# Twenty-eight copies of old value rows move from the prompt attention to the routing's queries, and from GpSimd to ScalarE

## The reference

```
p = modulate(rmsnorm(x)) @ w_in                 # q, k, v of two attention groups
oa = differential attention (softmax pair)      # prompt: causal; samples: paged past
ob = dilated window attention, three windows    # prompt; samples: past of 2048 rows
x += gate * ([norm(oa), ob] @ w_o)
q = modulate(rmsnorm(x)) @ peer_wq              # PEER: 8 heads, two halves of 128
s = q . keys; top 16 of each half, top 16 of the sums   # the routing
x += gate * sum over chosen experts of softmax * gelu(x . u[e]) * v[e]
y = rmsnorm(x)
k_win_sample = concat(state_k_win, kb)[:, 4:]   # the window state, moved by 4 rows
v_win_sample = concat(state_v_win, vb)[:, 4:]
```

## Time and profile before

| | |
|---|---|
| median of 3 runs | 4041.88 us (4033.55 to 4056.06) |
| the profiled execution | 4036.62 us |
| its span in the trace | 4034.8 us |
| busy: TensorE, weight load, VectorE, ScalarE, GpSimd | 82%, 72%, 69%, 34%, 42% |
| `prompt_attn`, 399.49 to 719.24 us | TensorE busy 240.7, VectorE 207.4, ScalarE 182.2 of 319.8 us; DMA 0.53 |
| queries, sparse turns, 1251.5 to 1387.4 us | TensorE busy 107.0 of 135.9 us; VectorE 0; DMA 0.34 |
| queries, dense turns, 1387.4 to 1537.5 us | TensorE busy 133.0, VectorE 133.7 of 150.1 us; DMA 0.34 |

### The profile page before, as it was taken

How to read it: one execution, slowest core, us unless ns; L and a number is a source line. 1 busy time by engine, 2 the same in 40 slices (tenths; PEclk the granted TensorE clock), 3 DMA queues, 4 the chain that set the end, 5 groups by cost and what they waited for, 6 DMA issues and landing times. The chain is left out here.

```text
span 4034.8 us, 59078 instructions
## 1 busy us (share of the span) xinstructions
PE 3311.0 (82%) x20585; PEld 2890.3 (72%) x20585; DVE 2778.2 (69%) x5881; ACT 1357.6 (34%) x3190; POOL 1709.0 (42%) x1341
## 2 busy tenths in 40 slices
PE   6999688566686892666589999999999999999994
PEld 3677455211376792555489999999999999999993
DVE  3223676100231199999779998999999889999885
ACT  3010466000221111887633333333333333333331
POOL 1010000000212441888765665665565565565560
PEclk7999799777788996776699999999999999999997
DMA  6632546999422331787598998998988988898983
GB/s 232 221 124 74 172 148 212 357 412 406 161 72 77 99 115 42 200 240 205 141 329 318 330 325 303 326 331 311 326 319 314 334 316 314 320 322 307 328 300 148
DMA packets 389552, 1001.89 MB, mean 248 GB/s; under 512 B 187044, under 2 KB 232975, under 8 KB 325688
## 3 DMA queue, kind: packets, MB, share of 16 engines
q1 hardware_dynamic: 323768, 491.18, 35.9%
q0 software_dynamic: 62656, 469.86, 32.2%
q10 hardware_dynamic: 2944, 38.77, 2.6%
HBM read 914.75 MB, written 152.04 MB: 264 GB/s over the span
## 5 line engine op out<-in xcount | busy, mean ns | idle before, releaser
L2174 DVE CUSTOM_DVE_ANT_0 e_uv<-e_uv,e_h 128x1024 f32<-128x1024 f32 x416 | 721.7, 1735 | 73.8 <-DMA e_uv<-peer_uv,k_g_idx 73.1
L2243 POOL DMA_INDIRECT e_uv<-peer_uv,k_g_idx x416 | 521.1, 1253 | 540.4 <-DVE e_pY L2186 496.8
L1475 PE MATMUL e_po<-e_ph,e_vh 128*128 128x320 f32 x2048 | 646.3, 316 | 59.2 <-DVE k_OT L2218 55.1
L1475 PE MATMUL e_pa<-k_hi_d,e_uh 128*128 128x320 f32 x2048 | 638.4, 312 | 50.7 <-POOL e_ul L2234 37.5
L1476 PE MATMUL e_po<-e_pl,e_vh 128*128 128x320 f32 x2048 | 633.3, 309 | 0.0
L1477 PE MATMUL e_po<-e_ph,e_vl 128*128 128x320 f32 x2048 | 633.3, 309 | 0.0
L1477 PE MATMUL e_pa<-k_hi_d,e_ul 128*128 128x320 f32 x2048 | 633.2, 309 | 0.0
L1476 PE MATMUL e_pa<-k_lo_d,e_uh 128*128 128x320 f32 x2048 | 633.1, 309 | 0.0
L2186 DVE SCALAR_TENSOR_TENSOR e_pY<-e_uv,e_wts,e_pY 128x1024 f32<-128x1024 f32 x412 | 526.0, 1277 | 0.0
L1475 PEld LDWEIGHTS e_po<-e_ph,e_vh 128*128 128x128 f32 x2048 | 384.8, 188 | 83.7 <-DVE k_OT L2218 71.3
L1475 PEld LDWEIGHTS e_pa<-k_hi_d,e_uh 128*128 128x128 f32 x2048 | 384.8, 188 | 62.0 <-issue 46.0
(11 more groups left out here) (305 smaller groups left out, 5889.7 us busy)
## 6 DMA issues: line engine op xcount, KB each, us to landing
k_kv<-kv_pages SPq DMA_DIRECT2D x128, 512.0 KB, 7.0
s_kv<-kv_state SPq DMA_DIRECT2D x32, 2048.0 KB
e_v<-peer_uv SPq DMA_DIRECT2D x128, 512.0 KB
e_u<-peer_ut SPq DMA_DIRECT2D x126, 512.0 KB, 6.1
s_g<-r_G SPq DMA_DIRECT2D x10, 4096.0 KB
k_OT<-s_g SPq DMA_DIRECT2D x128, 320.0 KB
v_win_sample<-state_v_win POOLq DMA_DIRECT2D x28, 1168.0 KB, 10.0
k_win_sample<-state_k_win ACTq DMA_DIRECT2D x28, 1168.0 KB
```

Source lines behind the costliest of these rows:

```text
L1475: nc.tensor.matmul(out, lhs_hi, rhs_hi, start=start, stop=False)
L2174: nc.vector.tensor_tensor_reduce(uv[:, r, 0:D], uv[:, r, 0:D], h[:], 1.0, 0.0, ALU.mult, ALU.add, dots[:, r:r + 1]).then_inc(row_dotted, 1)
L2243: nc.gpsimd.indirect_dma_start(uv[:, s % RING], None, io["peer_uv"], bass.IndirectOffsetOnAxis(ap=keep.g_idx[:, s:s + 1], axis=0),).then_i ...
```

## The change

GpSimd's program in `prompt_attn` falls away with its two semaphores. In the queries of `peer_route`, ScalarE issues share x of the values at the end of turn x, behind `scores_away(x - 1)`, for x from 0 to 27. Nobody waits for these until the end of `finish`, where SyncE already waited for the 28 of the keys and now waits for 56.

```diff
@@ prompt_attn
-        win_out = [nc.alloc_semaphore(f"a_win_out{u}") for u in range(2)]
...
-            @block.gpsimd
-            def _(pool):
-                with pool.Fori(0, WIN_SHARES // 2) as i:
-                    for u in range(2):
-                        copy_window(pool, io, "v", 2 * i + u).then_inc(win_out[u], 16)
-                        pool.wait_ge(win_out[u], 16 * i + 16)
@@ peer_route, ScalarE
                     queries_away(x)
                     if x:
                         scores_away(x - 1)
+                    if x < WIN_SHARES:
+                        copy_window(act, io, "v", x).then_inc(keep.win_out, 16)
                     if x in (NHC + 6, NHC + 11):
                         exps(ND if x == NHC + 6 else ND + 1)
@@ finish, SyncE
-                sp.wait_ge(keep.win_out, 16 * WIN_SHARES)
+                sp.wait_ge(keep.win_out, 2 * 16 * WIN_SHARES)
```

## The result

| | before | after |
|---|---|---|
| median | 4045.75 us (4 runs, 4033.55 to 4056.06) | 4181.97 us (4 runs, 4163.93 to 4200.73) |
| ratio | | 1.0338 (1.0271 to 1.0406) |
| profiled span | 4034.8 us | 4195.9 us |

The prediction was 4082 us, in a range of 4044 to 4122. The way was right, but the time lies outside the range: the loss is three to four times the one forecast. The profiled execution of after lies in the upper part of its runs, so its parts sum to 161 us, not to 136.

The account below looks back on a forecast made before the run. The queries were held bound by a ring of TensorE, GpSimd and the weights load. VectorE 53 us late less 10 gained gave +43 on 4036.62, 4079.6; plus 2, 4082 us, own range 4060 to 4105, with neighbours 4044 to 4122.

Parts of the forecast that it names:

- The gain: Prompt attention without its 28 copies: 6.4 us saved at the stage's end, 3.5 at its start, together 10 (6 to 13).
- The ring: Queries: TensorE waits for GpSimd, GpSimd for weights; 16.4 us per two sparse turns; a later load delays both equally.
- Eight engines for 6.7 us a share: Queries: each value share holds about 8 of 16 engines for 6.7 us and leaves the others free.
- h = 4 us: Queries: lateness of each weights load that waits for the rest of a share; 4 us, with 0 and 7.8 as ends.
- The meeting at 568 us: Prompt attention: an `a_qk` load meeting a copy landed after 14.7 us, its twin after 6.7 to 7.1; worst lateness 7.8.
- Turns 1 to 15: Sparse turns of the queries: 7 rounds, each 4.6 us longer including slower clock, 32 us in all.
- Turns 16 to 22: Queries: 3 rounds, each 5.0 us longer, 15 us; ScalarE's exponential of turn 22 and VectorE late by 47.
- Turns 22 to 27: Queries: 2.5 rounds, 12.5 us; exponential of turn 27 late by 59.5, VectorE by 53 after 6.4 of play.
- Turns 27 to 31: End of the queries: no share in turns 28 to 31, nothing added; first dense tile's load stays hidden.
- The load passes between the packets: Rival, queries: engines alternate, so the load loses one packet, 1.3 us; +5 in all, 4042 us; chance 0.16.
- The eight engines fill up: Rival, queries: 18.7 us of engine work against rounds of 16.4 to 17.4, queue runs behind; +91, 4128 us; chance 0.14.
- The share fills engines that are idle: Rival, queries: DMA at 0.34 leaves room, loads hardly late, not slower; 4027 to 4031 us without lateness; chance 0.08.

Follow-up runs that it names:

- e3: Kernel after with the same bytes in 32 shares of 511 rows of one sequence, each on sixteen engines; 4091.53 us, 1.0127 of before.
- e2: Kernel after with every second value share left out, 14 shares remaining; 4119.35 us, 1.0195 of before.
- e9: Kernel after with the shares issued by SyncE directly ahead of each turn's weights, instead of by ScalarE; 4127.23 us, 1.0226 of before.
- e4: Kernel after with 32 shares on sixteen engines, issued by SyncE directly behind each turn's weights; 4032.29 us, 0.9988 of before.
- e6: Kernel after with each share in 256 pieces of 4.7 KB instead of 40 of 30 KB, same eight engines; 4123.18 us, 1.0207 of before.

## Why the prediction was wrong

- **The gain.** 6.4 at the end and 3.5 at the start were forecast, 6.6 and 6.2 measured, and 3.8 more between, where nothing was forecast. At the start of the queries 11.7 us were left of the stage's 16.6, counted from the start of the prompt attention, where 10 was forecast. The two ends were rightly seen; that the sum came so near is partly luck, since 3.8 us unforeseen came in and 4.9 went again.
- **The ring.** That GpSimd waits for the weights and TensorE for GpSimd, and that a late load makes a round later by as much, is what the trace shows: the rounds took 15.6 us on average before and 30.3 after (turn 1 to turn 15), 14.7 more, and the load was later by 13.4 on average. VectorE's waits for ScalarE at turns 22 and 27 came as said. This part of the mechanism was right.
- **Eight engines for 6.7 us a share.** Held: 7.4 engines at work on the shares, and e3 against the kernel after.
- **h = 4 us: the step that failed.** The load was said to be late by the rest of one share, with 7.8 as the upper end from one meeting in the prompt attention. It was late by 16.0 us in the first sparse round and by 12.4 to 13.4 in the others, two whole shares. Two things were missed. First, a share ahead costs its whole 6.65 us, with no head start (e2: 7.2 a share; e9: late by one share, rounds of 23.8 us). The forecast let the load be in when the share is through, at 1280.7; but the load's own packets on those engines come only then, as the 0.43 MB between 1278 and 1281 us show. Second, the share of the next turn, issued 4.1 us after the load, was served ahead of it as well: 16.0 to 17.2 us from issue to use in the kernel after, against 10.2 to 10.7 in e9, where that share is behind the load in one queue. The meeting at 568 us had this form already: SyncE's queue was alone on the engines from 568 to 572 us, the share's packets came only then, and the rest of the load was still held up until 578. But GpSimd waited there for each share before the next, so two were never queued, and the bound taken from there could not hold this case.
- **The sum, term by term.** Turns 1 to 15: +32 forecast, +103 measured (109.0 to 211.9 us); 94 of it is the lateness of the loads; of the other 9, for which 4 were set, some is the slower clock. Turns 16 to 22: +15 against +22. Turns 22 to 27: +12.5 against +43. The weights of turns 23 and 27 took 21.0 and 20.0 us here (6.3 and 6.5 before): in SyncE's queue the 1024 KB of finished scores stand directly ahead of them, and the forecast had no term for them. Turns 27 to 31: 0 against +10, and the load of the first dense tile was no longer hidden (1.66 us of wait). VectorE late by 53 against 155.
- **The rivals.** "The load passes between the packets", to which I gave 0.16, had the taking of turns right and the price wrong. Against it I held the meeting at 568 us; but between 576 and 578.4 us 12 packets of the share's queue went beside 15 of SyncE's, which is turn-taking too. The load does not lose one packet, it loses one for each packet of its queue up to its own last, and these are more than a share or two have (37 for a turn on each engine, against 5 a share). "The eight engines fill up" came nearest in its number, 4128 us, and was still short; its ground did not hold, since the shares were through before the next round began (8 packets, 0.04 MB of ScalarE's queue between 1278 and 1281 us). "The share fills engines that are idle" is wrong for this place, but e4 comes near it: with the share behind the load the engines carry it for 8.5 us of queries.

## What to carry to other kernels

Before a transfer is moved beside a ring of loads, look at what it stands in front of, on the engines that it uses: here a bulk copy cost a waited-for load its full length when it was issued ahead, and little when it was issued behind in the same queue; on another queue a copy issued behind the load cost its full length too. Where an engine takes turns between queues, compare packets and not bytes: a load of many small packets, with small stores ahead of it, lets as many long packets of a copy go first. Count how many bulk copies can be queued before the load is served, and bound the price by their sum, not by one meeting in a stage where they were issued one at a time. A low mean DMA share (0.34 here) says nothing of a load that is on the path.

## What was not expected of the hardware

- A load already issued on SyncE's queue waited for a share issued 4.1 us after it on ScalarE's: over 4 us the engines gave 46.2% to ScalarE's queue and 1.4% to SyncE's. The service was uneven in time and bytes and not in packets: 199 packets against 201 over 5 us with pieces of 4.7 KB (e6), 23 against 23 over 5 us with pieces of 30 KB. Pieces of 4.7 KB took the queries from 464 to 402 us.
- The copy of 1168 KB over 8 engines cost the queries 6.4 us each, the one of 1022 KB over 16 engines 2.5 us, and 1.75 us in pieces of 4.7 KB.
